# One wait fewer on POOL: the decay of two arrays in the pipelined RWKV-7 scan

## The reference, cut to what matters

```python
def rwkv7_scan(r, w, k, v, a, bb):
    def step(S, inp):
        r_t, w_t, k_t, v_t, a_t, b_t = inp
        sa = jnp.einsum('zdhij,zdhj->zdhi', S, a_t)
        S = S * w_t[..., None, :] + sa[..., :, None] * b_t[..., None, :] + v_t[..., :, None] * k_t[..., None, :]
        y = jnp.einsum('zdhij,zdhj->zdhi', S, r_t)
        return S, y
...
    k_dir = (k[:, :, None].astype(f32) * (1.0 + (iclr - 1.0) * k_a.astype(f32))).reshape(b, L, N_DIR, H, N)
...
    y = rwkv7_scan(both(r_h), both(decay.reshape(b, L, N_DIR, H, N)), both(k_dir),
                   both(v_h), both(-kk), both(kk * iclr_h))
```

## Time and profile before

| | us |
|---|---|
| median of 3 runs (lowest, highest) | 2604.74 (2601.93, 2605.55) |
| the profiled execution's own time | 2606.3 |
| its span in the trace | 2604.2 |
| PE busy | 2475.9 |
| PE weight loads busy | 2051.4 |
| DVE busy | 1222.2 |
| POOL busy | 820.3 |
| ACT busy | 716.1 |

### The profile page before, as it was taken

One profiled execution on the slowest core, in us unless ns is written; L12 is line 12 of the kernel. 1 busy time (PEld: TensorE's weight loads), 2 busy tenths in 40 slices (PEclk: granted clock), 3 DMA queues, 4 the chain that ended last, 5 costly groups with the idle time before them and its releaser, 6 DMA issues. The chain is left out here.

```text
span 2604.2 us, 63663 instructions
## 1 busy us (share of the span) xinstructions
PE 2475.9 (95%) x28048; PEld 2051.4 (79%) x28048; DVE 1222.2 (47%) x2468; ACT 716.1 (27%) x1759; POOL 820.3 (31%) x627
## 2 busy tenths in 40 slices
PE   7999999999999599999999889999999999999997
PEld 6785568888888488888888767878888888888885
DVE  4105660000565356566666565554444444444446
ACT  5015661011111355545545432210111001110013
POOL 3322212222332233334333265022433223323234
PEclk9999999999999799999999989999999999999998
DMA  6110011111110100000000062211111111111114
GB/s 165 45 33 18 1 50 66 73 73 67 39 41 25 42 5 4 4 4 4 4 4 4 4 245 86 89 57 47 35 41 41 33 33 49 41 41 33 33 65 145
DMA packets 39086, 123.10 MB, mean 47 GB/s; under 512 B 11424, under 2 KB 11424, under 8 KB 37664
## 3 DMA queue, kind: packets, MB, share of 16 engines
q1 hardware_dynamic: 38816, 119.06, 13.5%
HBM read 96.24 MB, written 20.97 MB: 45 GB/s over the span
## 5 line engine op out<-in xcount | busy, mean ns | idle before, releaser
L2042 DVE TENSOR_TENSOR ff_f<-ff_f,ff_ps 128x512 f32<-128x512 f32 x300 | 205.4, 686 | 173.7 <-PE ff_ps L98 173.6
L1959 ACT ACTIVATE ff_rl<-ff_ps 128x512 f32<-128x512 f32 (+1 forms) x96 | 50.5, 526 | 755.0 <-PE ff_ps L98 755.0
L2061 DVE TENSOR_TENSOR ff_sq<-ff_rl 128x512 f32<-128x512 f32 (+1 forms) x96 | 127.2, 1325 | 269.8 <-ACT ff_rl L1959 269.5
L998 DVE TENSOR_TENSOR sc_q<-sc_ps,sc_cs 128x128 f32<-128x128 f32 x400 | 98.9, 282 | 200.5 <-PE sc_ps L422 198.0
L1828 POOL TENSOR_TENSOR ff_wd0h<-ff_wdr,params 128x1024 fp32r<-128x1024 f32 x16 | 30.3, 1892 | 462.6 <-DMA ff_wdr<-in_w_down 462.6
L757 ACT ACTIVATE sc_xy<-sc_ps 128x256 f32<-128x256 f32 x320 | 115.6, 386 | 174.7 <-PE sc_ps L438 170.9
L438 PE MATMUL sc_ps<-sc_xy,sc_q 64*64 64x64 f32 x3200 | 150.8, 220 | 7.0 <-DVE sc_q L998 4.4
L98 PE MATMUL ff_ps<-hh,ff_wu0h 128*128 128x512 f32 (+1 forms) x384 | 136.6, 356 | 5.1 <-issue 5.1
L98 PE MATMUL ff_ps<-hl,ff_wu0h 128*128 128x512 f32 (+1 forms) x384 | 136.4, 355 | 0.0
L98 PE MATMUL ff_ps<-hh,ff_wu0l 128*128 128x512 f32 (+1 forms) x384 | 136.4, 355 | 0.0
L98 PE MATMUL ff_ps<-hh,ff_wu1h 128*128 128x512 f32 (+1 forms) x384 | 136.0, 354 | 0.0
(11 more groups left out here) (306 smaller groups left out, 7049.7 us busy)
## 6 DMA issues: line engine op xcount, KB each, us to landing
ff_wur<-in_w_up SPq DMA_DIRECT2D x32, 512.0 KB, 3.5
ff_wdr<-in_w_down SPq DMA_DIRECT2D x32, 512.0 KB, 4.4
gwr<-in_w_in SPq DMA_DIRECT2D x31, 512.0 KB, 3.2
gm_dram<-gp_gm SPq DMA_DIRECT2D x8, 1280.0 KB, 4.4
ff_m<-gm_dram SPq DMA_DIRECT2D x16, 640.0 KB, 7.5
fr_x<-in_x SPq DMA_DIRECT2D x10, 512.0 KB, 4.8
ff_xs<-in_x SPq DMA_DIRECT2D x10, 512.0 KB, 4.1
x_dram<-ff_xo SPq DMA_DIRECT2D x10, 512.0 KB, 2.9
```

The lines of the kernel that those rows point to most:

```text
L998: nc.vector.tensor_tensor(Q1[g][:, :, :], q_out[g], joins[:, l, :].rearrange("p (u t) -> p u t", u=2), ALU.mult).then_inc(q_ready, 1)
L1959: nc.scalar.activation(rl[v % 2][:, 0:tn], ps[:, b, 0:tn], ACT.Relu).then_inc(relu, 1)
L2042: nc.vector.tensor_tensor(own, own, ps[:, 4 + v % 4, :], ALU.add).then_inc(added, 1)
L2061: nc.vector.tensor_tensor(sq[v % 2][:, 0:tn], rl[v % 2][:, 0:tn], rl[v % 2][:, 0:tn], ALU.mult).then_inc(squared, 1)
```

## The change

In `prepare`, the second wait ahead of the decay of b and k goes; the wait for `neg` stays, and no instruction is added, removed or put elsewhere on any engine.

```diff
@@ -295,8 +295,6 @@
                     own.mark(nc.gpsimd.tensor_tensor(both_blocks(kd[:, :], i), both_blocks(kd[:, :], i), k,
                                                      ALU.add))
                 pool.wait_ge(neg_ready, q + 1)
-                if q:
-                    pool.wait_ge(x1_ready, (q - 1) * GR + 3)
                 nc.gpsimd.tensor_tensor(b, b, neg[:, :, :], ALU.mult)
                 own.wait()
                 nc.gpsimd.tensor_tensor(k, k, neg[:, :, :], ALU.mult)
```

## The result

The changed kernel takes 2625.06 us (median of 4 runs, 2623.55 to 2629.41), the kernel before 2605.14 us (4 runs, 2601.93 to 2607.76) in the same comparison. The ratio is 1.0078, with a 95% interval from 1.0063 to 1.0093: 0.8% slower, 16 to 24 us. I had forecast 2618.3 us, 0.5% slower, with 2623.0 as the upper end of the range. The direction and the mechanism of the delay hold; the size is 6 to 7 us more than I reckoned and 2 us above that upper end.

A forecast was written before the change was run, and what follows sets the result against it. PE's stream sets the pace, with gaps where the ring PE, DVE, PE, ACT is late. Gain 0 and 13.6 us of collisions on 2606.3 give 2619.9, or 2618.3 us against the median 2604.7; range 2608.5 to 2623.

The forecast's parts named there:

- What goes away: nothing on the path.: POOL's 22.1 us idle ahead of b's decay only moves ahead of a, which awaits the later transpose; gain 0.
- Two POOL operations onto two DVE operations.: Without the hold, b's and k's decays meet DVE lines 897 and 901; each waits out one POOL operation plus 0.15 us.
- Price of one collision, and its sum.: Step 19: DVE 1.89 us late, 1.81 reaches PE; over 11 colliding steps 13.6 us.
- slack: Part of DVE's delay that PE doesn't feel at the mask: 0.08 us in step 19, 2.0 of 15.7 in all.
- I take the loss whole.: PE's side work and level 3 run in order behind the mask, so the delay left after slack counts fully.
- waits that I don't follow: Upper-end allowance: a late ring PE, DVE, PE, ACT could cost a fifth more; with table-step collisions 18 us.
- 1 (one of two waits): DVE gets both operations in after the first decay, so only one wait per collision: +5.2 us, 2610; chance 0.10.
- 2 (POOL restarts too late): POOL takes over 0.9 us from copy to b's decay and misses DVE: no change, 2604.7 us; chance 0.09.
- 3 (the hold is on the path): Arrays a and r and PE's Gram products come sooner: at most 22.1 us faster, 2583; chance 0.02.
- 4, more than the sum: The four table steps collide too, or the ring loses more than the delay: 2621 to 2626 us; chance 0.12.
- a table step: Steps 3, 8, 13, 18: ACT loads a table ahead of Exp, neg is late, POOL comes behind DVE; cost 0.

The follow-up runs named there:

- psum_free: The changed kernel (no hold) with DVE's two operations reading the Gram product in PSUM, system-matrix mask left out; 2600.29 us against 2604.55 before, ratio 0.9988.
- before_again: The kernel before, unedited, executed once more to see what repeats; 2608.13 us.
- after_again: The changed kernel, unedited, executed once more to see what repeats; 2622.69 us.
- fill_last: free_last plus five matmuls of constants on PE ahead of its wait for the mask in steps 9, 14 and 19; 2615.08 us, ratio 1.0035 to before.
- free_last: The kernel before with the hold given up in steps 4, 9, 14 and 19 alone; 2612.9 us, ratio 1.0039.
- hold_last: The kernel before with the hold kept only in steps 4, 9, 14 and 19; 2611.6 us against 2604.55, ratio 1.0037.
- bonus_late: The kernel before, hold kept, with the bonus term's two long POOL operations released later, mostly by DVE's learning-rate operation; 2598.16 us against 2605.26, ratio 0.9970.
- clear: bonus_late, and in steps 5, 10 and 15 POOL decays k first, then holds b until DVE has done group 3; 2593.18 us against 2605.26 before.

## Why the prediction was right or wrong

**What goes away: nothing on the path.** Right. The idle time ahead of the decay moved to the place ahead of a, and a and r waited for the same transpose.

**Two POOL operations onto two DVE operations.** Right in kind, shown by psum_free: without the second SBUF input the change costs nothing. Of the two statements of the Trainium skill that I weighed, the one of "SBUF — State Buffer", section Who interferes with whom, is the one that this kernel bears out for operations with two SBUF inputs; with the one of "Advanced Engine Details and Errata", section VectorE Performance Modes, alone the sum would have been 0 against 20 us measured. Small deviations: in step 2 DVE's first operation slipped in ahead, so that only the second waited. In step 3, which I had at 0, neg came 0.55 us earlier against the factor than before, and both collided, with 0.56 us of idle time of PE. In before_again neg stands at that earlier place too, so this is no effect of the change; the trace that I read was late there. The release took the 0.15 us that I used: in step 19 POOL's decays ended at 1454.71 and 1456.00, DVE's operations at 1454.87 and 1456.15. POOL's decays grew from 1273 to about 1300 ns: where DVE had got in just before, most took 1.32 us, and elsewhere 1.27, so POOL waits too.

**Price of one collision, and its sum.** Right: 13.6 us of idle time for PE reckoned, 13.2 found, and 14.7 in after_again; in the undisturbed steps 7, 11, 12, 16 and 17 the added time was 6.2 us against 5.5. In steps 9, 11, 12, 14, 16, 17 and 19 the idle time was 10.1 us where I had 10.3. In the early steps the sum came out by luck: 2, 4 and 6 gave 1.24 us where I had 2.91, 3 and 7 gave 1.95 where I had 0.41. In step 7 of the one trace I read PE came late to the mask, behind an idle time of 0.89 us of its own, and I took that lateness for slack; before_again has no such idle time, and took 30.88 us for the step instead of 31.80.

**"I take the loss whole."** This is the step that failed, from the other side than I guarded. I let the idle time of PE cost itself and no more, and put "waits that I don't follow" at a fifth. In steps 9, 14 and 19 PE's clock fell to 1.2 GHz behind the idle time, and they cost 11.6 us where 5.2 was reckoned. fill_last shows the cause: the same delay with a busy PE brings them to 5.0. The trace of before held a sign of this: at its idle time of 1.93 us in step 19 PE was at half clock for 3.4 us, and the prediction gives the clock of 1170 to 1330 us alone. The missing term is 6.4 us in the first trace; 13.6 + 6.4 = 20.0, beside 19.9 between the medians. That the match is so close is luck in part, since steps 2 to 6 gave 0.3 us where I had 2.9, and the stages behind the scan 1.3 more.

**The rivals.** 1 (one of two waits) held in step 2 alone. 2 (POOL restarts too late) and 3 (the hold is on the path) are out: POOL went from copy to decay with no gap, and no wait for r appeared in the loop. 4, more than the sum, is what came. Of its two reasons one held in part: step 3, a table step, collided, with 0.56 us, and 8, 13 and 18 did not. The rest is the clock, which it did not name.

**Open.** What decides whether the clock falls behind an idle time. Behind the mask in steps 9, 14 and 19 it fell in all nine cases of the changed kernel's two traces and free_last (1.47 to 1.97 us idle), and in steps 7, 11, 12, 16 and 17 of the changed kernel's two traces and hold_last in none of fifteen (1.16 to 1.42 us). The length alone does not decide it: at the idle time of 1.93 us for a join in step 19 the clock fell in before, and not in before_again and hold_last. Of eleven idle times of 1.39 to 1.40 us for a join in steps 9 and 14, in seven of the traces, five had a drop behind them and six had none. Steps 9, 14 and 19 also have another kind of side work behind the mask (line 511, two rows) than the five (line 500); I did not separate that from the length, but the drops at a join came without it.

Open is also in part by what the medians of fill_last and free_last hid the gain of 5.9 us. Some of it is the clock elsewhere: of the 4.8 us by which steps 0 to 6 differ, 0.73 and 1.33 stand in steps 1 and 5, where fill_last was at half clock for some 3 us more each, and behind the scan it was so for 8 us more. Steps 2 and 3 gave 2.4 us at full clock in both. Steps 0 to 6 differ by 2.0 us between two executions of one kernel, and whether a part of the 4.8 belongs to the program was not tried.

## What to carry to other kernels

A wait that looks idle may keep an engine out of another one's way: before a hold is removed, lay the two engines' timelines over each other, and see which operations of the other would run beside what is let go. Where PE sets the pace, price a new idle time of PE twice, once as delay and once with a stretch behind it at the lower clock, which may or may not come, and look in the trace, over its whole length, whether such idle times were followed by one. Take slack from more than one trace. And search for the collisions that are there already: the longest instance beside the median of each DVE line finds them in a minute, and here bonus_late and clear together were worth 12 us.

## What the runs showed of the hardware that I had not expected

- The granted clock of TensorE fell from 2.4 to 1.2 GHz behind single idle times of 1.47 to 1.97 us in a stream otherwise over 90% busy, for 3.4 or 6.8 us at a time, behind the same mask in three steps of two executions of one kernel and one of another. In five other steps, behind 1.16 to 1.42 us, it stayed. But an idle time of 1.93 us was followed by no drop in two runs and accompanied by one in a third, and one of 0.80 us was followed by a drop where 0.79 and 0.88 were not.
- Five dummy matmuls of 128 columns in the idle time kept it up behind the mask in all three steps, and saved 5.9 us in three steps.
- A tensor_scalar of one SBUF tensor, 128x512 float32, which takes 0.41 us, took 2.89 us when it came 0.3 us after the start of a POOL operation of 2.9 us, until that one was over; so it is not only operations with two SBUF inputs that wait. By the Trainium skill, "SBUF — State Buffer", section Who interferes with whom, a tensor_scalar can run in a two-port mode and then contends with GpSimd; the trace agrees, at 2.89 us in place of 0.41.
- POOL waits as well: most of its decays took 1.32 us instead of 1.27 where DVE had got in between.
- The same two DVE operations with one input in PSUM took 0.291 to 0.293 us in psum_free, also beside POOL.
